# Summing 28 of 64 modulation units with one-column products on TensorE instead of VectorE

## The reference, cut to what matters

```python
c_act = jax.nn.silu(c)
for l in range(DEPTH):
    mod = c_act @ ada_w[l] + ada_b[l]
    shift, scl, gate_res = jnp.split(mod[:, None, :], 3, axis=-1)
    h = _rms(x, norm_g[l]) * (1.0 + scl) + shift
    z = h @ w_in[l]
    ...
    x = x + gate_res * ((y * jax.nn.silu(g)) @ w_out[l])
```

## Time and profile before

| | us |
|---|---|
| time, median of 3 runs (1017.04 to 1020.48) | 1017.18 |
| time of the profiled execution | 1017.85 |
| its span, first to last instruction | 1016.1 |
| PE busy / DVE busy / ACT busy in the span | 955.8 / 835.2 / 437.3 |

### The profile page before, as it was taken

One profiled execution on the slowest core, in us unless ns is written; L12 is line 12 of the kernel. 1 busy time (PEld: TensorE's weight loads), 2 busy tenths in 40 slices (PEclk: granted clock), 3 DMA queues, 4 the chain that ended last, 5 costly groups with the idle time before them and its releaser, 6 DMA issues.

```text
span 1016.1 us, 20238 instructions
## 1 busy us (share of the span) xinstructions
PE 955.8 (94%) x7728; PEld 945.8 (93%) x7728; DVE 835.2 (82%) x1244; ACT 437.3 (43%) x693; POOL 46.7 (5%) x63
## 2 busy tenths in 40 slices
PE   5197799999999999999999999999999999999997
PEld 5197789999999999999999999999999999999997
DVE  4898987987899778887877898888999986878842
ACT  4122125434555444333344444444446555743331
POOL 1000000011010000000000000000010100000000
PEclk9997798999999999999999999999999999999999
DMA  8999988989777888899857755544445555588961
GB/s 337 339 325 360 324 296 316 321 287 369 290 275 243 279 285 287 312 359 362 312 189 269 242 196 180 189 137 162 150 162 180 167 172 199 196 309 307 342 220 41
DMA packets 71094, 261.32 MB, mean 257 GB/s; under 512 B 7904, under 2 KB 8032, under 8 KB 70768
## 3 DMA queue, kind: packets, MB, share of 16 engines
q1 hardware_dynamic: 68544, 250.86, 70.0%
q0 software_dynamic: 2480, 9.50, 2.6%
HBM read 256.07 MB, written 4.19 MB: 256 GB/s over the span
## 4 chain that ended last, share of the span: by engine, by line
PE 77%; DVE 14%; DMA 4%; issue 3%; ACT 2%; SPq 0%; DVEq 0%; POOL 0%; ACTq 0%; POOLq 0%
PE bank L707 20%; PE bank L708 19%; PE bank L709 19%; DVE acc L1038 6%; DVE wlo L1027 3%; PE bank L809 3%; DMA ada<-ada_units 3%; PE bank L812 3%; PE bank L811 3%; PE bank L724 1%; PE bank L726 1%; PE bank L727 1%; PE bank L777 1%; DVE X L1105 1%; ACT whi L400 1%
## 5 line engine op out<-in xcount | busy, mean ns | idle before, releaser
L400 ACT ACTIVATE whi<-raw 128x1024 fp32r<-128x1024 f32 x282 | 297.2, 1060 | 447.6 <-PE bank L709 338.5
L1027 DVE TENSOR_TENSOR wlo<-raw,whi 128x1024 fp32r<-128x1024 f32 x282 | 341.4, 1224 | 91.9 <-ACT whi L400 91.3
L707 PE MATMUL bank<-hhi,whi 128*128 128x256 f32 x1168 | 337.1, 289 | 2.3 <-ACT T L619 0.9
L708 PE MATMUL bank<-hlo,whi 128*128 128x256 f32 x1168 | 330.4, 283 | 0.0
L709 PE MATMUL bank<-hhi,wlo 128*128 128x256 f32 x1168 | 330.3, 283 | 0.0
L1038 DVE SCALAR_TENSOR_TENSOR acc<-ada,cact,acc 128x1024 f32<-128x1024 f32 x176 | 226.1, 1285 | 33.0 <-DMA ada<-ada_units 16.5
L707 PEld LDWEIGHTS bank<-hhi,whi 128*128 128x128 f32 x1168 | 223.9, 192 | 5.7 <-issue 3.8
L708 PEld LDWEIGHTS bank<-hlo,whi 128*128 128x128 f32 x1168 | 224.1, 192 | 0.1
L709 PEld LDWEIGHTS bank<-hhi,wlo 128*128 128x128 f32 x1168 | 223.8, 192 | 0.0
L707 PE MATMUL bank<-ghi,whi 128*128 128x256 f32 x512 | 147.9, 289 | 0.0
L708 PE MATMUL bank<-glo,whi 128*128 128x256 f32 x512 | 144.9, 283 | 0.0
(11 more groups left out here) (166 smaller groups left out, 1070.1 us busy)
## 6 DMA issues: line engine op xcount, KB each, us to landing
raw<-w_slabs SPq DMA_DIRECT2D x282, 512.0 KB, 4.9
ada<-ada_units SPq DMA_DIRECT2D x192, 512.0 KB, 6.3
X<-xT SPq DMA_DIRECT2D x1, 2048.0 KB, 7.6
x_dram<-X POOLq DMA_DIRECT2D x4, 512.0 KB, 5.4
outT<-X POOLq DMA_DIRECT2D x4, 512.0 KB, 5.0
V<-pool_w POOLq DMA_DIRECT2D x1, 1024.0 KB, 6.2
U<-xT POOLq DMA_DIRECT2D x2, 512.0 KB, 9.8
V<-xT POOLq DMA_DIRECT2D x2, 512.0 KB, 7.4
```

The costliest lines, as they stand in the source:

```text
L400: act.activation(whi[:, slot], raw[:, slot], ACT.Copy).then_inc(hi_done, 1)
L707: mm(out, whi[:, s, k, :], ahi[:, c, :], start=(c == 0), stop=False)
L708: mm(out, whi[:, s, k, :], alo[:, c, :], start=False, stop=False)
L1027: dve.tensor_tensor(wlo[:, s], raw[:, s], whi[:, s].bitcast(F32), ALU.subtract)\
```

## The change

1. Of the units 0 to 63, 28 are no longer added by DVE: every unit with `n % 4 == 3`, and from unit 16 on also those with `n % 4 == 1`. PE sums them straight from the slot: eight products of a 128x128 block of `ada` with one column of `cact` (`sum_units`), which accumulate in PSUM. For pieces 0 and 2 and the second half of piece 3 this is bank O, for piece 1 and the first half of piece 3 bank M. The 36 other units stay on DVE, and the sum over `acc` (`add_sums`, eight products a piece as before) is accumulated on top.
2. `ada_done` becomes one counter for each of the four slots, `ada_used`. A slot with `n % 4 == 3` now comes free when PE has used it.
3. On PE the sums stand between the products: in piece 0 between the `x_stat`, in pieces 1 to 3 mostly two units before each `wide_chunk`. `keep_warm` in this stage goes away. PE waits for `mod_done` of an earlier piece before it writes into the same bank again.
4. The lists of ACT and DVE for slabs 0 to 11 are rewritten: `hi` and `lo` of some slabs stand later, and DVE's units are interleaved with them one by one.

The loads, their sizes and their order on SyncE stay the same.

```diff
+def on_pe(unit):
+    return unit < FIRST * UNITS and (unit % 4 == 3 or (unit % 4 == 1 and unit >= UNITS))
...
                     slot = (n + u) % 4
                     unit = n + u if t is None else n + u + 4 * t
-                    sp.wait_ge(ada_done, unit + 1)
+                    uses = (n + u) // 4
+                    if uses:
+                        sp.wait_ge(ada_used[slot], uses if t is None else uses + t)
...
             hi(0, None)
-            hi(1, None)
             root(0, QT)
             act.wait_ge(spread, 1)
             act.activation(DS[:, 0, 0:SEQ], XB[:, 0:SEQ], ACT.Copy).then_inc(r_copied, 1)
-            for g in range(3):
-                upper_h(0, range(GROUP * g, GROUP * (g + 1)))
-                hi(3 * g + 2, None)
-                hi(3 * g + 3, None)
-                if g < 2:
-                    hi(3 * g + 4, None)
+            hi(1, None)
+            upper_h(0, range(0, 4))
+            for w in (2, 3):
+                hi(w, None)
+            upper_h(0, range(4, 8))
+            for w in (4, 5, 6):
+                hi(w, None)
+            upper_h(0, range(8, 12))
+            for w in (7, 8):
+                hi(w, None)
             upper_h(0, range(12, 14))
-            hi(10, None)
+            for w in (9, 10):
+                hi(w, None)
             upper_h(0, range(14, 16))
             hi(11, None)
...
+            def sum_units(units):
+                for n in units:
+                    slot, p, u = n % 4, n // UNITS, n % UNITS
+                    pe.wait_ge(ada_in[slot], 16 * (n // 4 + 1))
+                    if p < 3:
+                        for j in range(HC):
+                            ins = mm(sum_bank(p, j)[:, j:j + 1], ada[:, slot, j * P:(j + 1) * P], cact[:, u:u + 1],
+                                     start=(j == 0 and n in (3, 17, 33)), stop=False,
+                                     skip_group_check=True)
+                    else:
+                        j0 = HC // 2 * (u // 8)
+                        for r in range(2):
+                            k = 2 * (u % 8) + r
+                            for j in range(HC // 2):
+                                at = PIECE // 2 * r + j * P
+                                ins = mm(sum_bank(p, j0)[:, j0 + j:j0 + j + 1], ada[:, slot, at:at + P],
+                                         cact[:, k:k + 1], start=(j == 0 and k == 2), stop=False,
+                                         skip_group_check=True)
+                    ins.then_inc(ada_used[slot], 1)
+            def add_sums(p, j0, j1, after):
+                pe.wait_ge(ada_used[after % 4], after // 4 + 1)
+                for j in range(j0, j1):
+                    ins = mm(sum_bank(p, j)[:, j:j + 1], acc[:, p % 2, j * P:(j + 1) * P], ones[:, 0:1],
+                             start=False, stop=True, skip_group_check=True)
+                return ins
             pe.wait_ge(const, 3)
-            for i in range(KC):
+            pe.wait_ge(c_ready, 1)
+            for i in range(8):
                 x_stat(i)
+            sum_units((3,))
+            for i in range(8, 14):
+                x_stat(i)
+            sum_units((7,))
+            for i in range(14, KC):
+                x_stat(i)
+            sum_units((11,))
             spread_token(0)
-            for p in range(3):
-                if p:
-                    pe.wait_ge(ada_done, UNITS * p + 12 + 4)
-                    keep_warm(24, M)
-                reduce_piece(p)
-                for c in range(GROUP * p, GROUP * (p + 1)):
-                    if c == 11:
-                        pe.wait_ge(ada_done, UNITS * 3 + 8 + 4)
-                        pe.wait_ge(mod_done, 3)
-                        for j in range(4):
-                            ins = reduce_part(3, j, half=True)
-                        ins.then_inc(half_sum, 1)
-                    wide_chunk(0, U0, c)
+            sum_units((15,))
+            add_sums(0, 0, HC, 14).then_inc(mod_sum, 1)
+            for p in (1, 2):
+                if p == 2:
+                    pe.wait_ge(mod_done, 1)
+                sum_units((UNITS * p + 1, UNITS * p + 3))
+                wide_chunk(0, U0, 4 * p - 4)
+                sum_units((UNITS * p + 5, UNITS * p + 7))
+                wide_chunk(0, U0, 4 * p - 3)
+                sum_units((UNITS * p + 9, UNITS * p + 11))
+                wide_chunk(0, U0, 4 * p - 2)
+                sum_units((UNITS * p + 13, UNITS * p + 15))
+                add_sums(p, 0, HC, UNITS * p + 14).then_inc(mod_sum, 1)
+                wide_chunk(0, U0, 4 * p - 1)
+            pe.wait_ge(mod_done, 2)
+            sum_units((49, 51))
+            wide_chunk(0, U0, 8)
+            sum_units((53, 55))
+            add_sums(3, 0, HC // 2, 54).then_inc(half_sum, 1)
+            wide_chunk(0, U0, 9)
+            wide_chunk(0, U0, 10)
+            pe.wait_ge(mod_done, 3)
+            sum_units((57, 59))
+            wide_chunk(0, U0, 11)
             wide_chunk(0, U0, 12)
+            sum_units((61, 63))
+            add_sums(3, HC // 2, HC, 62).then_inc(mod_sum, 1)
             wide_chunk(0, U0, 13)
-            pe.wait_ge(ada_done, UNITS * 4 + 4)
-            for j in range(4, HC):
-                reduce_part(3, j)
...
-                    dve.wait_ge(ada_done, unit + 4)
+                    acc_settled(first + u, t)
                     dve.scalar_tensor_tensor(acc[:, p % 2, :], ada[:, slot, :], cact[:, bass.ds(k, 1)],
-                                             acc[:, p % 2, :], ALU.mult, ALU.add).then_inc(ada_done, 1)
+                                             acc[:, p % 2, :], ALU.mult, ALU.add).then_inc(ada_used[slot], 1)
...
-            for p in range(3):
+            dve.wait_ge(acc_zero, 1)
+            add_units(0, 3, None)
+            add_units(4, 3, None)
+            add_units(8, 3, None)
+            lo(0, None)
+            dve.wait_ge(stat_done, KC)
+            rsqrt(0, QT, M[:, 0:QT], D_MODEL)
+            token_diag()
+            add_units(12, 1, None)
+            lo(1, None)
+            add_units(13, 2, None)
+            dve.wait_ge(r_copied, 1)
+            for p in (1, 2):
                 dve.wait_ge(acc_zero, p + 1)
-                add_units(UNITS * p, 4, None)
-                if p:
-                    group_of_h(p - 1)
-                add_units(UNITS * p + 4, 4, None)
-                if p:
-                    lo(3 * p - 1, None)
-                add_units(UNITS * p + 8, 4, None)
+                add_units(UNITS * p, 1, None)
+                group_of_h(p - 1)
+                add_units(UNITS * p + 2, 1, None)
+                if p == 2:
+                    lo(4, None)
+                add_units(UNITS * p + 4, 1, None)
+                add_units(UNITS * p + 6, 1, None)
+                lo(3 * p - 1, None)
+                add_units(UNITS * p + 8, 1, None)
+                add_units(UNITS * p + 10, 1, None)
                 lo(3 * p, None)
-                add_units(UNITS * p + 12, 2, None)
-                lo(3 * p + 1, None)
-                add_units(UNITS * p + 14, 2, None)
-                if p == 0:
-                    dve.wait_ge(stat_done, KC)
-                    rsqrt(0, QT, M[:, 0:QT], D_MODEL)
-                    token_diag()
-                    dve.wait_ge(r_copied, 1)
+                add_units(UNITS * p + 12, 1, None)
+                add_units(UNITS * p + 14, 1, None)
             dve.wait_ge(acc_zero, 4)
-            half_units(48, 4)
+            half_units((48,))
             group_of_h(2)
-            half_units(52, 4)
+            half_units((50,))
+            lo(7, None)
+            half_units((52, 54))
             lo(8, None)
-            half_units(56, 4)
+            first_half()
+            half_units((56,))
             lo(9, None)
-            first_half()
-            half_units(60, 2)
+            half_units((58, 60))
             lo(10, None)
-            half_units(62, 2)
+            half_units((62,))
...
```

More of the change, by code:

```diff
@@ L48 @@
               (62, 70, 1), (70, 72, 2), (110, 111, 2), (112, 113, 2), (115, 117, 1), (121, 125, 1), (125, 132, 2))
+FIRST = 4
 H_PIECE = {0: (0, 1, 2, 3), 1: (4, 5, 8, 9)}
@@ L161, in build @@
         z_free = [sem(f"z_free{i}") for i in range(2)]
-        ada_done = sem("ada_done")
+        ada_used = [sem(f"ada_used{i}") for i in range(4)]
+        c_ready = sem("c_ready")
         acc_zero = sem("acc_zero")
@@ L237, in flat, with sum_bank @@
             return ap.rearrange("p a t -> p (a t)")
+        def sum_bank(p, col):
+            return M if p == 1 or (p == 3 and col < HC // 2) else O
         def bank_uses(w, t):
@@ L245, in _ @@
             sp.sem_inc(lo_done, 4)
-            sp.sem_inc(ada_done, 4)
             sp.dma_start(par[:], params).then_inc(par_in, 16)
@@ L752, in spread_token, with reduce_part @@
                 ins.then_inc(spread, 1)
[L754 to L758, removed]
+            def reduce_part(p, j):
+                if j == 0:
```

(22 more changed lines are left out.)

## The result

| | us |
|---|---|
| changed kernel, median of 4 runs (1047.42 to 1050.85) | 1049.14 |
| kernel before, median of 4 runs beside it (1017.04 to 1020.48) | 1018.05 |
| ratio | 1.0302, 95% interval 1.0276 to 1.0328 |
| span of the profiled execution | 1047.4 |

The account below looks back on a forecast made before the run. DVE bounds the first stage, with PE waiting for `hlo`; afterwards PE is the bound. The profiled 1017.85 + 3.8 (piece 0 and PE's list) + 22 (clock falls) = 1043.6, against the median 1043 us; range 1019 to 1051.

Parts of the forecast that it names:

- DVE is relieved and PE becomes the bound: First stage, pieces 1 and 2: DVE needs 22 us a piece instead of 33, PE 32.5; waits for `hlo` go.
- A unit costs 1.70 us at full clock, 3.41 at the low one: A unit's 16 one-column instructions on PE: 106 ns apart at full clock, 213 ns at the low clock.
- Piece 0 costs 1.1 us: Start of first stage: `add_sums` ends at 47.5 instead of 46.35, costing 1.1 us (-2.7 to +3.7).
- PE's list of 120.6 us, against 118.0: First stage behind piece 0: PE's units, `add_sums`, wide products and first rise total 120.6 us, so +2.7.
- The falls, 11 x 2.0 = 22 us: Pieces 1 to 3: clock falls in or behind most of 11 blocks, 2.0 us each; bounds 14 and 33 us.
- the first rise: First wide products behind piece 0: 5.07 us with 24 products at 213 instead of 120 ns, costing 2.2 us.
- What would show it: First-stage profile signs: DVE near 70% busy, clock mean 0.7 to 0.8, falls in most blocks, end at 180 to 198 us.
- the chance of 0.76: First stage: chance that the clock falls in most blocks, giving 1035 to 1051 us.
- The clock holds: Rival, first stage: clock stays up through blocks after its first rise; only 3.8 us remain, 1021 us; chance 0.13.
- One-column products count as work in both directions: Rival, from 9.5 us on: PE reaches 2.4 GHz during `x_stat`, stage ends 5.3 us earlier, 1012 us; chance 0.07.
- The slots: Rival, first stage: loads wait for PE's slots and PE waits too, up to 20 us, near 1055; chance 0.04 (with more falls).

Follow-up runs that it names:

- Experiment 2: Kernel before, with blocks of 16 or 8 unused one-column products ahead of each of slabs 43 to 47: 1043.13 us (1.0275) and 1027.35 us (1.0070).
- experiment 5: Changed kernel with 16 units on PE: 1031.28 us; also with 128 columns: 1026.53; then one DVE line moved: 1023.36; changed kernel, seven of eight products omitted: 1019.5.

## Why the prediction was right

It gave 1043 us, 1019 to 1051; measured were 1049.14.

- **DVE is relieved and PE becomes the bound.** Right. PE waits for `hlo` no more, and the stage has 0.7 us of waits for units behind piece 0.
- **A unit costs 1.70 us at full clock, 3.41 at the low one.** The second is right: 3.57 us for one at 33.08, with the end of its last instruction. The first is a little low: 3.49 for two at 102.59. The 106 ns were a mean over the sixteen instructions at 274.59, of which the second comes 28 ns behind the first and all others 112 ns apart. In a block of 32 the mean is 109, and the switch to the wide products takes the rest back.
- **Piece 0 costs 1.1 us.** It costs 2.1: `add_sums` ends at 48.5, inside the bounds of 43.7 to 50.1.
- **PE's list of 120.6 us, against 118.0.** Right in the main and some 2 us short: 400 one-column instructions at full clock are 2.4 us longer at 112 ns than at 106. The run with 128 columns and no falls seems to confirm 120.6 (its stage behind piece 0 takes 124.3 us, 48.5 to 172.8, with 2.3 of waits), but that is partly luck: there the first block raised the clock, which saves 3.4 us of the low-level time in the list.
- **The falls, 11 x 2.0 = 22 us.** The sum is right, the terms are not, and that they cancel is luck. There are 9 falls with 5.7 us at the low level behind each (windows of half a microsecond, summed, give 51 us). At the low level a wide product loses 0.44 of its time and a one-column product half, so 51 us lose some 23, 2.6 a fall.
- **Missing.** In the changed kernel the stage behind piece 0 takes 146.6 us, and 146.6 - 120.6 - 23 leaves 3. Of these 2.4 are the 112 ns, and about 1 is the wait for a unit in the block at 119.89 (0.7 idle, and a slow instruction behind it); the first rise was 0.4 cheaper. Together with piece 0 (+1.0), the falls (+1) and a kernel before that ran 0.9 slower beside it, this is the 6 us by which it fell short.
- **What would show it.** Two of the signs came otherwise. DVE is busy for 50% of the stage from 47 us on (73.8 of 148.1 us), not for near 70: 22 of 32.5 us a piece would be 68%, but the falls that the prediction itself expected make the pieces longer. And the clock's mean is 0.83, not 0.7 to 0.8, because the record reads 1.00 until its first change at 59.1; with the 10.6 us before that at the low level, as the distances have it, the mean is 0.79.
- **What it rested on.** Both falls that the prediction read in the kernel before, at 80.1 and 151.8, came while PE stood idle, since 78.9 and since 150.7. They could not show that the clock falls on one-column products with a busy PE, and the chance of 0.76 was given without such a row. Experiment 2 supplies it.
- **The rivals.** *The clock holds* is refuted as a description of the change. Its price, 1021, was too low: with 128 columns the clock held, and the time was 1027.18, with the waits and the terms above on top. *One-column products count as work in both directions* is refuted, since the `x_stat` from 9.56 on are 213 ns apart as before. *The slots*: behind piece 0 there is one such wait of 0.7 us in the changed kernel, which fits that PE itself is the bound and covers them. I named that cover, but gave the rival 0.04 as if it were a small matter; experiment 5 shows that without it waits take back nearly all that a lighter PE could give. And with a full clock the change would not have paid either: that is the run with 128 columns, 10 us above the kernel before.

By the Trainium skill ("TensorE: Matmul & The Clock Gate", section "Part 1: The HAM clock gate"), read as a rule on idleness, the clock would have stood. The trace does not agree in that reading: it fell nine times with PE busy for 145.7 of 146.9 us.

## What to carry to other kernels

Work with few columns on TensorE is paid twice: by its own time, some 110 ns for an instruction with one column against 120 for one with 256, and by the clock of what stands beside it. If it must be there, keep blocks short against the dense work (1.7 us beside 5.8 us held, 3.4 us did not), never mix it evenly with dense work at the start of a stretch, or give it columns: 128 instead of one cost no time here and took away every fall. And before work is moved from a bound engine to one with pauses, add up what the second will do at both clocks, and ask whose slots it will then free: here PE's waits for `hlo` were 20.5 us and its `keep_warm` 11.0, and the 24 units put in behind piece 0 are 42 us at full clock.

## What the runs showed of the hardware that was not expected

- A mix of 36 wide and 32 one-column instructions, evenly spread, did not raise TensorE's clock from 1.2 GHz: for 140 us in one run (55.8 to 195.5) and for 110 us in another (85.8 to 196.0), with PE busy almost throughout. The record of the first reads 1.00 all that time, since it has no change before 204.3; only the distances (213 ns) tell. In chunk 9, with 16 one-column instructions to 36 wide ones, it rose.
- Products with 128 equal columns from one column of `cact` (a broadcast operand) raised the clock within 4.2 us (49.43 to 53.67), where 13.8 us of one-column products had not. A block of 32 of them took 3.49 us, as long as with one or 64 columns.
- Between one-column and wide products the records show a late and an early start (200 ns instead of 120 behind the first wide one, 30 instead of 112 behind the first one-column one, at 2.4 GHz). They cancel: at 1.2 GHz, 68 instructions with some twelve changes each way took 14.51 us, 213 ns each (70.34 to 84.85). A mean over a short block, as the 106 ns here, is too low for a long one.
- With 128 columns and 16 units, the clock fell four times (at 69.2, 82.9, 106.8 and 134.1 us), each time in or just behind a pause of PE of 2.3 to 3.1 us; with 28 units and 128 columns no pause of PE reached 1 us behind piece 0, and nothing fell.
